# Two-stage attention in a transformer chain: the reciprocal softmax sums of uncombined head pairs are spread through memory by SP's DMAs instead of by TensorE and ScalarE

## The reference

```
p = softmax(where(mask, s, -inf), axis=-1)     # s: scores plus a bias, 512 x 512, causal
o = p @ v                                      # 64 columns a head
```

## Time and profile before

| | |
|---|---|
| median of 3 runs | 2996.83 us |
| the profiled execution's own time | 2995.95 us |
| its span, first to last instruction | 2993.9 us |
| granted TensorE clock, mean | 0.995 |
| PE busy | 2940.9 us (98%) |
| DVE busy | 1652.1 us (55%) |
| ACT busy | 1143.4 us (38%) |
| GpSimd busy | 151.2 us (5%) |
| first attention stage, 1302 to 1366 us | PE 61.41, DVE 49.84, ACT 48.28, GpSimd 26.41 us of 64 |
| second attention stage, 1918 to 1991 us | PE 62.49, DVE 56.51, ACT 52.48, GpSimd 18.09 us of 73 |

### The profile page before, as it was taken

The page is one execution under the profiler, slowest core; times in us unless marked ns, Lnnn a source line. Parts: engine busy times, 40 slices in busy tenths (PEclk is TensorE's granted clock), DMA queues, the critical chain, the costliest instruction groups (busy, mean ns, idle before and its releaser), DMA issues. The chain is left out here.

```text
span 2993.9 us, 37543 instructions
## 1 busy us (share of the span) xinstructions
PE 2940.9 (98%) x14364; PEld 2446.7 (82%) x14364; DVE 1652.1 (55%) x2334; ACT 1143.4 (38%) x1582; POOL 151.2 (5%) x301
## 2 busy tenths in 40 slices
PE   8999989999999999999999999999999999999999
PEld 6888888888888888868888888678888887888887
DVE  7747476544653336875433357766535567754453
ACT  4223243222432225464322235554423347443232
POOL 0101001000010001040000000110000002000000
PEclk9999999999999999999999999999999999999999
DMA  7747417544362322251322222422332222223231
GB/s 284 261 146 244 136 55 240 176 158 158 120 211 98 99 98 97 86 171 68 113 98 94 96 84 92 142 80 85 105 99 94 95 85 84 94 90 106 92 100 69
DMA packets 100914, 367.08 MB, mean 123 GB/s; under 512 B 11120, under 2 KB 11680, under 8 KB 100784
## 3 DMA queue, kind: packets, MB, share of 16 engines
q1 hardware_dynamic: 77616, 277.08, 27.5%
q0 software_dynamic: 23168, 88.17, 8.7%
HBM read 363.03 MB, written 2.18 MB: 122 GB/s over the span
## 5 line engine op out<-in xcount | busy, mean ns | idle before, releaser
L986 DVE TENSOR_TENSOR wl<-raw,wh 128x1024 fp32r<-128x1024 f32 x501 | 610.4, 1228 | 985.2 <-ACT wh L541 984.8
L541 ACT ACTIVATE wh<-raw 128x1024 fp32r<-128x1024 f32 x501 | 524.0, 1055 | 1205.9 <-PE PS L1679 1156.1
L1679 PE MATMUL PS<-HH,wh 128*128 128x512 f32 x2432 | 948.0, 390 | 12.0 <-DVE HL L1549 10.4
L1679 PE MATMUL PS<-HL,wh 128*128 128x512 f32 x2432 | 946.9, 389 | 0.0
L1679 PE MATMUL PS<-HH,wl 128*128 128x512 f32 x2432 | 946.9, 389 | 0.0
L1679 PEld LDWEIGHTS PS<-HH,wh 128*128 128x128 f32 x2432 | 457.1, 188 | 109.2 <-DVE HL L1549 7.2
L1679 PEld LDWEIGHTS PS<-HH,wl 128*128 128x128 f32 x2432 | 456.9, 188 | 95.2
L1679 PEld LDWEIGHTS PS<-HL,wh 128*128 128x128 f32 x2432 | 457.1, 188 | 94.5
L1679 PE MATMUL PS<-AH,wh 128*128 128x512 f32 x848 | 330.0, 389 | 0.4 <-ACTq L887 0.4
L1679 PE MATMUL PS<-AH,wl 128*128 128x512 f32 x848 | 329.9, 389 | 0.0
L1679 PE MATMUL PS<-AL,wh 128*128 128x512 f32 x848 | 329.9, 389 | 0.0
(11 more groups left out here) (269 smaller groups left out, 3075.6 us busy)
## 6 DMA issues: line engine op xcount, KB each, us to landing
raw<-in_stream SPq DMA_DIRECT2D x501, 512.0 KB, 3.3
acc<-in_stream POOLq DMA_DIRECT2D x86, 512.0 KB, 4.8
piece<-in_stream POOLq DMA_DIRECT2D x42, 512.0 KB, 4.9
arena<-in_stream SPq DMA_DIRECT2D x16, 512.0 KB, 11.3
TBa<-negcum POOLq DMA_DIRECT2D x8, 640.0 KB, 5.1
TBa<-in_alibi POOLq DMA_DIRECT2D x8, 640.0 KB, 4.7
TBb<-negcum POOLq DMA_DIRECT2D x4, 640.0 KB, 4.5
piece<-negcum POOLq DMA_DIRECT2D x4, 640.0 KB, 5.6
```

Of the source, the lines that this page charges most:

```text
L541: F(wh[:, r, :], raw[:, r, :], ACT.Copy).then_inc(hi_done, 1)
L986: TT(wl[:, r, :], raw[:, r, :], wh[:, r, :].bitcast(F32), ALU.subtract).then_inc(lo_done, 1)
L1679: mm = MM(PS[g % 2][:, j, :], l, x, start=(first and i == 0), stop=(last and i == 2), skip_group_check=after_halves)
```

## The change

For each of the 12 plain pairs, the eight spreading matmuls and ACT's copy are removed. In their place, SP stores `rz` (128 x 8 floats) to a small array in memory with the positions made contiguous, waits for that store (`rz_out`), and then loads each head's 512 reciprocals into its 64 partitions of `OT_flat` (two DMAs with a repeating source, `rz_in`). DVE's multiplication waits for `rz_in`. Plain pairs' reciprocals are moved to the start of DVE's turn, ahead of the scores of rounds 0 and 1. Before a load may write `OT`, SP waits for the earlier user of that buffer (`o_turned`, `o_ready`). SP's chunk loop is cut in three, so that these DMAs stand at their place in the program, after the chunk loads that can be issued before the stage.

```diff
--- before.py
+++ after.py
@@ -298,6 +298,7 @@
             return PS[(g + b // 4) % 2][:, b % 4, :]
 
         negcum = nc.dram_tensor("negcum", (HEADS, SEG[4]), F32, kind="Internal").ap()
+        recips = [nc.dram_tensor(f"recips{n}", (2, 4, 128), F32, kind="Internal").ap() for n in range(2 * PAIRS - COMBINED)]
 
 
         raw_full = [sem(f"raw_full{r}") for r in range(RING)]
@@ -341,8 +342,8 @@
 
         pv_done, pv_read, sub_normed, o_turned, o_hi, o_ready = (sem(n) for n in (
             "pv_done", "pv_read", "sub_normed", "o_turned", "o_hi", "o_ready"))
-        bias_masked, rz_ready, combined, sub_summed, rz_spread, rz_copied = (sem(n) for n in (
-            "bias_masked", "rz_ready", "combined", "sub_summed", "rz_spread", "rz_copied"))
+        bias_masked, rz_ready, combined, sub_summed, rz_out, rz_in = (sem(n) for n in (
+            "bias_masked", "rz_ready", "combined", "sub_summed", "rz_out", "rz_in"))
         pool_step, sub_root = (sem(n) for n in ("pool_step", "sub_root"))
 
         lam_dot, lam_exp, sp_neg, sp_exp = (sem(n) for n in (
@@ -431,16 +432,48 @@
                     sp.dma_start(maskf[:, :], A["mask"]).then_inc(rest_in, 16)
                     sp.dma_start(bones[:, :], A["bones"]).then_inc(rest_in, 16)
             sp.dma_start(bands[:, 0:NBAND], A["params"][:, NCOL:NCOL + NBAND]).then_inc(bands_in, 16)
-            rounds = NCH // RING
-            if rounds > 2:
-                with sp.Fori(2, rounds) as i:
-                    for r in range(RING):
-
-                        sp.wait_ge(lo_done, i * RING + (r + 1 - RING))
-                        load(i * RING + r, r)
-            for c in range(max(rounds, 2) * RING, NCH):
-                sp.wait_ge(lo_done, c + 1 - RING)
-                load(c, c % RING)
+
+            def load_chunks(a, b):
+                first, last = min(-(-a // RING), b // RING), b // RING
+                for c in range(a, min(first * RING, b)):
+                    sp.wait_ge(lo_done, c + 1 - RING)
+                    load(c, c % RING)
+                if first < last:
+                    with sp.Fori(first, last) as i:
+                        for r in range(RING):
+
+                            sp.wait_ge(lo_done, i * RING + (r + 1 - RING))
+                            load(i * RING + r, r)
+                for c in range(max(last * RING, a), b):
+                    sp.wait_ge(lo_done, c + 1 - RING)
+                    load(c, c % RING)
+
+            def spread_sums(pair, i, fox, st):
+
+                n = before(pair, 1, 0)
+                row, slot = recips[n], 2 * (pair % 2)
+                sp.wait_ge(rz_ready, pair + 1)
+                sp.dma_start(row.rearrange("u q p -> p u q"), rz[:, slot:slot + 2, :],
+                             allow_slow_non_contiguous=True).then_inc(rz_out, 16)
+                sp.wait_ge(rz_out, 16 * (n + 1))
+                if not fox:
+                    sp.wait_ge(o_turned, min(i - 1, COMBINED))
+                if i >= 2 and plain(fox, i - 2):
+                    sp.wait_ge(o_ready, st["o"] + FINISHED[fox][i - 2])
+                for u in range(2):
+                    sp.dma_start(OT_flat(pair)[64 * u:64 * u + 64, :],
+                                 row[u:u + 1, :, :].rearrange("u q p -> u (q p)").broadcast_to((64, S)))\
+                        .then_inc(rz_in, 16)
+
+            done = 2 * RING
+            for st in plan:
+                if st["kind"] == "attend":
+                    load_chunks(done, st["c"] + RING + 3)
+                    done = st["c"] + RING + 3
+                    for i in range(PAIRS):
+                        if plain(st["fox"], i):
+                            spread_sums(st["a"] // 2 + i, i, st["fox"], st)
+            load_chunks(done, NCH)
             rows = out[0].rearrange("(a p) c -> p a c", p=128)
             sp.wait_ge(out_rows, 1)
             sp.dma_start(rows[:, :, 0:512], XOUT[:, :, 0:512]).then_inc(out_done, 16)
@@ -810,11 +843,6 @@
                     for i in range(PAIRS + 2):
                         if 1 <= i < PAIRS:
                             pair_exp(p0 + i, i, (0,))
-                        if 2 <= i <= PAIRS + 1 and plain(fox, i - 2):
-                            act.wait_ge(rz_spread, before(p0 + i - 1, 1, 0))
-                            if not fox:
-                                act.wait_ge(o_turned, min(i - 3, COMBINED))
-                            F(OT_flat(p0 + i - 2), attend_bank(7, g), ACT.Copy).then_inc(rz_copied, 1)
                         if 1 <= i < PAIRS:
                             pair_exp(p0 + i, i, (1,))
                         if 4 <= i < 4 + COMBINED and not fox:
@@ -1272,6 +1300,8 @@
                 slot = 2 * (pair % 2)
                 dve.wait_ge(p_ready, 8 * pair + 8)
                 if plain(fox, i):
+                    if before(pair, 1, 0) >= 2:
+                        dve.wait_ge(rz_out, 16 * (before(pair, 1, 0) - 1))
                     nc.vector.reciprocal(rz[:, slot:slot + 2, :], Z[:, slot:slot + 2, :]).then_inc(rz_ready, 1)
                     return
                 link(nc.vector.reciprocal(rz[:, slot:slot + 2, :], Z[:, slot:slot + 2, :]))
@@ -1490,20 +1520,20 @@
                 elif kind == "attend":
                     p0, fox = st["a"] // 2, st["fox"]
                     for i in range(PAIRS + 2):
+                        if 1 <= i <= PAIRS and plain(fox, i - 1):
+                            pair_sums(p0 + i - 1, i - 1, fox)
                         if 1 <= i < PAIRS:
                             pair_scores(p0 + i, i, fox, g, (0,))
                         if 1 <= i <= PAIRS and not plain(fox, i - 1):
                             pair_sums(p0 + i - 1, i - 1, fox)
                         if 1 <= i < PAIRS:
                             pair_scores(p0 + i, i, fox, g, (1,))
-                        if 1 <= i <= PAIRS and plain(fox, i - 1):
-                            pair_sums(p0 + i - 1, i - 1, fox)
                         if 2 <= i <= PAIRS + 1:
                             b = p0 + i - 2
                             dve.wait_ge(pv_done, b + 1)
                             if plain(fox, i - 2):
                                 o = OT_flat(b)
-                                dve.wait_ge(rz_copied, before(b + 1, 1, 0))
+                                dve.wait_ge(rz_in, 32 * before(b + 1, 1, 0))
                                 TT(o, attend_bank(6, g), o, ALU.mult).then_inc(pv_read, 1)
                             else:
                                 if i >= 4:
@@ -1866,16 +1896,6 @@
 
                 bank, slot, col = attend_bank(6, g), 2 * (pair % 2), 128 * tile_of(fox, i)
                 pe.wait_ge(pt_act, before(pair + 1, 2, 2))
-                if plain(fox, i):
-                    pe.wait_ge(rz_ready, pair + 1)
-                    if not fox:
-                        pe.wait_ge(pt_vec, before(pair, 3, 1) + 2)
-                    for qt in range(4):
-                        for u in range(2):
-                            mm = MM(attend_bank(7, g)[64 * u:64 * u + 64, 128 * qt:128 * qt + 128],
-                                    rz[:, slot + u, qt:qt + 1].broadcast_to((128, 64)), ident[:, :],
-                                    start=True, stop=True, skip_group_check=True)
-                    mm.then_inc(rz_spread, 1)
                 pe.wait_ge(pt_vec, before(pair + 1, 3, 1))
                 if plain(fox, i):
                     for kt in range(4):
```

## The result

| | before | after |
|---|---|---|
| median | 2996.99 us (4 runs, 2995.99 to 2997.54) | 3062.25 us (4 runs, 3059.36 to 3067.05) |
| ratio, 95% interval | | 1.022 [1.0206, 1.0233] |
| profiled execution, span | 2993.9 us | 3061.3 us |
| granted TensorE clock, mean | 0.995 | 0.984 |
| last multiplication of the first stage starts | 1365.40 us | 1410.28 us |

The kernel became 65 us slower. The forecast of no change was wrong, the range missed it by 50 us, and the rival with the slow store came true, at its dear end. The last two rows say where: 44.9 us are lost in the first attention stage, 22.6 more by the end of the second, and nothing after it (the spans differ by 67.4 us).

What follows compares the result with a forecast made beforehand. TensorE, busy nearly the whole span, was taken to set the pace. Gains of 0.7 + 1.3 + 2.1 = 4.1 us, taken as 4.0, gave 2991.9 us profiled, 2992.8 us as median; range 2988 to 3012.

Steps and rivals of the forecast that it cites:

- The forecast of no change: Whole kernel: store and loads hidden, 2992.8 us, a gain within the 0.2% counted as no change; chance of within 0.61.
- the rival with the slow store: SP becomes the bound above a 7.2 us landing: +21 us at 9 us, +64 us (3061) at 12.5 us; chance 0.23.
- the price of the store: SP's store of 1024 4-byte pieces: 3.9 us taken, from 1.6 plus 64 x 0.035 us; upper end 12.5 us.
- What goes: Attention turns: spread removed, ceiling 11.0 us; a turn shrinks by 0.8 us, five turns by 4.0 us, before GpSimd's limit.
- The loop of 7.26 us: First stage: the round through ACT, DVE and TensorE that sets the next limit on a turn, against 8.07 us before.
- the cap of 2.7 us: End of first stage: GpSimd's masks let the last scores come at most 2.7 us earlier, not 4.0.
- Delay of the bias loads: GpSimd's bias loads share DMA with SP's transfers: 0.4 us a turn over five pairs, bounds 0 and 3.0 us.
- Is it hidden: Detour of 6.4 us against 9.9 us of cover mid-stage, 6.4 at the first stage's end; hidden, with 2.4 us for loads.
- Ends and second stage: First stage's end gives 1.3 us; second stage 2.1 us, from two turns of 0.9 us and 0.15 us for either last spread.

Runs made afterwards that it cites:

- experiment 5: Changed kernel with the store's 1,024 4-byte pieces 64 bytes apart and the loads reading the weight stream: 2996.94 us, ratio 1.0002.
- experiment 2: Changed kernel with the store as 128 contiguous pieces of 32 bytes, so the loads bring reciprocals in a wrong order: 2993.88 us, ratio 0.9991.
- 10: Changed kernel with 4-byte pieces 8 bytes apart, eight of one partition in each 64 bytes; loads from the weight stream: 3024.23 us, ratio 1.0092.
- 13: Changed kernel with 4-byte pieces 8 bytes apart, eight of eight partitions in each 64 bytes; loads from the weight stream: 3011.93 us, ratio 1.0045.
- 18: Changed kernel storing identity values, each partition's eight pieces side by side in 32 bytes, partitions 64 bytes apart; loads from the weight stream: 3026.21 us, ratio 1.0099.
- experiment 1: Changed kernel without the stores and loads; DVE multiplies by whatever stands in `OT`: 2990.05 us, ratio 0.9978 against the kernel before.
- 4: Changed kernel without the store; the two loads a pair read a row of the weight stream: 2993.8 us, ratio 0.999.

## Why the prediction was wrong

**The step that failed is the price of the store**: "64 x 0.035 = 2.3, so 3.9 us." SP's waits are 10.9 us a store in the first stage (87.1 / 8). The 3.9 us are what 1,024 pieces cost that lie 64 bytes apart (3.8 us in experiment 5); the four small stores of the earlier trace rows on which the 35 ns rested say nothing of pieces laid side by side. The reason given for that end, "because the packets it rests on are the smallest there are", looked at the size of a packet and not at where it is written, and it is the place that decides: for the same pieces in the same number SP waits 10.9 us a store side by side and 4.5 us (36.2 / 8) at 64 bytes. The Trainium skill (DMA: Bandwidth & Descriptors, Rules for kernel authors) advised against the store, and rightly; but neither its floor of 10.5 ns a packet (an estimate of 2.7 us) nor its read-modify-write below 512 B says that the distance between the pieces counts, and the 32-byte pieces of experiment 2, also under 512 B, landed in 2.4 us.

**The rival was right, for half a right reason.** SP became the bound, seven of the eight pairs of the first stage paid, and its 3061 us at 12.5 us is within 1.3 us of the result. In part that is luck. The eight stores took 11.5 us on average from their issue to that of their loads. With this for the landing, its sum would be 7 x (11.5 + 0.8 - 8.07) = 30 in the middle, 11.5 + 2.5 - 6.4 = 8 at the first end, and about 14 for the second stage (between its 4 at 9 us and its 18 at 12.5): some 51, not 65. Of the other 14, about 8 lie in SP's turn, 13.4 us on average where its sum has 12.3, among them the 4.0 us for which SP stood for late reciprocals. What it didn't have is that the loads took 5.0 us at the median and up to 12.0 instead of 2.4, and that TensorE ran at 1.2 GHz after its long pauses (mean clock 0.82 from 1300 to 1420 us). How much of the 14 us goes back to each of the two wasn't separated. Its chance of 0.23 was too low: the bounds were 3.9 and 12.5 us, the kernel turned slow from 7.2, and no row favoured the lower end beyond the size of a packet. And 7.2 was too high: stores of 6.6 to 7.2 us (experiments 10, 13 and 18), for which its sum gives next to no loss, cost 15 to 30 us. In 10 DVE waits 14.7 us for loads in the first stage and 6.0 us for masks: slower loads and delayed biases belong to the same turn.

**What goes: right.** L1875 and L817 are gone from the groups. The loop of 7.26 us is the 7.27 us of one turn of experiment 1 (the two after it took 7.43 and 7.62); the first stage gave 4.6 us where 2.7 + 1.3 = 4.0 was forecast, and the whole 6.9 (medians) where 6.1 was named as the best end. GpSimd's mask held DVE in one turn for 0.84 us, as forecast, but the cap of 2.7 us was drawn too tight. It set the end of both masks against DVE's first read, and DVE needs the second head's mask only at its second read: that came at 1347.61 instead of 1350.97, 3.4 us earlier.

**Delay of the bias loads: right in kind, too small.** Priced at 5 x 0.4 = 2.0 us; experiments 2 and 4 show 3.8 us in the medians, and 3.5 and 2.3 us in the first stage of their traces. The loads alone make it; the store adds nothing if its pieces are long. Part of the reason for the low price was that the two queues take turns; in the changed kernel SP's loads, issued at 1352.25, show no packet before 1356 us, while GpSimd's queue moves 126 of its own from 1354 to 1356 us.

**Is it hidden: right on its condition.** With stores that land in 2.4 us DVE never waited for a load; at 3.8 us (experiment 5) three waits, 3.0 us in sum. The landing of 2.4 us for the loads was 3.0 beside a quick store (median; the slowest of 16 took 7.9).

**Ends and second stage.** Experiment 1's last multiplication of the second stage starts 2.6 us earlier than before; as its first one starts 1.8 us earlier, the stage after it gave 0.8 us. The first two multiplications lie 8.68 us apart instead of 9.56: the turn gave 0.88 us where 0.9 was forecast. The two ends gave nothing where 0.3 was forecast, and in experiments 2 and 4 these distances are the same within 0.02 us. The other turn, whose spread stood ahead of the first of these multiplications, can't be read apart, since that execution was 3.7 us above the median of its kernel; so the 2.1 us of the forecast are confirmed in one part, too high by 0.3 in another, and open in the rest.

## What to carry to other kernels

Before a scattered store is priced by its pieces, look at where they land: many 4-byte writes laid side by side in memory complete late, and neither the number of packets nor the share of busy DMA engines shows it. If rows must be turned, turn them on the chip and write long rows, or leave the detour out; and price a detour with its condition, here the point from which its queue becomes the bound, since both bounds of an unshown cost count until a row of the same pattern excludes one.

## What the runs showed of the hardware

- 1,024 writes of 4 bytes land in 3.5 to 4 us if at most four fall into each 64 bytes, in about 7 us with eight, in about 11 with sixteen; 512 writes with sixteen in 64 bytes are hardly quicker (SP's wait 78.0 us for eight stores against 87.1). Eight in 64 bytes with a kilobyte to the next group took 10.8 us, unexplained; whether the length that counts is 64 bytes or more is not shown.
- The packets of such a store are gone long before it is complete: none from 1360 to 1364 us (share 0.00), where SP could go on only at 1365.45. Other transfers suffer: bias loads on the other queue moved 32 packets in the four microseconds from 1350 to 1354 us, those to `TBa` land in 9.6 us instead of 5.1, and loads that SP issued before a store aren't reported complete for up to 12.0 us.
- TensorE, idle from 1355.2 us, was granted half its clock from 1358 us and kept it for the first work after the pause, from 1365.58 us to about 1371: 3.41 us for score rounds that took 2.00.
